# Third and fourth unit's loads behind the third block of ada, and one more row of two blocks summed on TensorE

## What is computed

```python
c_act = silu(c)
mod = c_act @ ada_w + ada_b                       # 1024 x 9216
sh1, sc1, g1, sh2, sc2, g2, sh3, sc3, g3 = split(mod, 9)
h = rms_norm(x, norm_ffn1) * (1 + sc1) + sh1
x = x + 0.5 * g1 * ((silu(h @ w_gate) * (h @ w_up)) @ w_down)
...                                               # token mixing, second feed-forward, last norm
```

## Time and profile before

| | |
|---|---|
| time, median of 3 runs | 1157.45 us (1156.35 to 1160.7) |
| time of the profiled execution | 1155.71 us |
| its span | 1153.6 us |
| PE busy | 1132.6 us, 98% of the span |
| DVE, ACT, POOL busy | 737.0, 493.1, 117.8 us |
| granted clock, mean over the span | 0.996 |

### The profile page before, as it was taken

The page is one execution under the profiler, slowest core; times in us unless marked ns, Lnnn a source line. Parts: engine busy times, 40 slices in busy tenths (PEclk is TensorE's granted clock), DMA queues, the critical chain, the costliest instruction groups (busy, mean ns, idle before and its releaser), DMA issues. The chain is left out here.

```text
span 1153.6 us, 17468 instructions
## 1 busy us (share of the span) xinstructions
PE 1132.6 (98%) x6378; PEld 989.6 (86%) x6378; DVE 737.0 (64%) x1167; ACT 493.1 (43%) x758; POOL 117.8 (10%) x115
## 2 busy tenths in 40 slices
PE   8999999999999999999999999999989999999997
PEld 6788888888888998888888888889889999978887
DVE  4766665666555666675555666757789898952332
ACT  5233332233222257665555665533545454532232
POOL 3301000000110001112011230001310101100000
PEclk9999999999999999999999999999999999999999
DMA  9567566557777425538246674341335445333331
GB/s 311 166 214 248 186 216 203 170 175 233 230 235 237 121 59 119 121 101 171 73 121 118 141 144 98 90 128 56 105 101 145 126 128 147 111 101 91 96 114 73
DMA packets 244174, 167.95 MB, mean 146 GB/s; under 512 B 6198, under 2 KB 224516, under 8 KB 244116
## 3 DMA queue, kind: packets, MB, share of 16 engines
q1 hardware_dynamic: 227188, 143.48, 41.6%
q0 software_dynamic: 16208, 21.33, 8.8%
q10 hardware_dynamic: 720, 2.36, 0.6%
HBM read 164.99 MB, written 16.05 MB: 157 GB/s over the span
## 5 line engine op out<-in xcount | busy, mean ns | idle before, releaser
L1893 PE MATMUL bank<-hH,wH 128*128 128x512 f32 (+1 forms) x976 | 355.1, 364 | 3.9 <-DVE hL L1283 3.4
L1895 PE MATMUL bank<-hH,wL 128*128 128x512 f32 (+1 forms) x976 | 351.2, 360 | 0.0
L1894 PE MATMUL bank<-hL,wH 128*128 128x512 f32 (+1 forms) x976 | 351.0, 360 | 0.0
L798 ACT ACTIVATE wH<-raw 128x1024 fp32r<-128x1024 f32 x131 | 135.8, 1037 | 351.2 <-PE bank L1895 348.4
L1217 DVE TENSOR_TENSOR wL<-raw,wH 128x1024 fp32r<-128x1024 f32 x131 | 156.7, 1196 | 201.3 <-ACT wH L798 200.4
L1893 PEld LDWEIGHTS bank<-hH,wH 128*128 128x128 f32 x976 | 184.1, 189 | 33.6 <-issue 5.4
L1895 PEld LDWEIGHTS bank<-hH,wL 128*128 128x128 f32 x976 | 184.0, 189 | 28.0
L1894 PEld LDWEIGHTS bank<-hL,wH 128*128 128x128 f32 x976 | 184.2, 189 | 26.3
L1893 PE MATMUL bank<-actH,wH 128*128 128x512 f32 (+1 forms) x316 | 120.7, 382 | 0.0
L1895 PE MATMUL bank<-actH,wL 128*128 128x512 f32 (+1 forms) x316 | 120.4, 381 | 0.0
L1894 PE MATMUL bank<-actL,wH 128*128 128x512 f32 (+1 forms) x316 | 120.4, 381 | 0.0
(11 more groups left out here) (276 smaller groups left out, 1932.6 us busy)
## 6 DMA issues: line engine op xcount, KB each, us to landing
adaw<-in_ada_w_dram SPq DMA_DIRECT2D x28, 1024.0 KB, 6.1
raw<-in_mix_w_in_dram SPq DMA_DIRECT2D x41, 512.0 KB, 3.9
raw<-in_ffn_w_down_dram SPq DMA_DIRECT2D x32, 512.0 KB, 4.0
raw<-in_ffn_w_gate_dram SPq DMA_DIRECT2D x25, 512.0 KB, 4.0
raw<-in_ffn_w_up_dram SPq DMA_DIRECT2D x25, 512.0 KB, 3.9
adas<-in_ada_w_dram SPq DMA_DIRECT2D x16, 512.0 KB, 8.2
raw<-in_ffn_w_down_dram SPq DMA_DIRECT2D x16, 384.0 KB, 4.2
wsum_d<-in_ffn_w_gate_dram POOLq DMA_DIRECT2D x8, 704.0 KB, 7.7
```

What stands on the lines that cost most here:

```text
L798: nc.scalar.activation(wH[s][:, :n * P], raw[s][:, :n * P], ACT.Copy).then_inc(hi_done, 1)
L1893: T.matmul(o, a[0], b[0], start=start, stop=False)
L1894: T.matmul(o, a[0], b[1], start=False, stop=False)
L1895: return T.matmul(o, a[1], b[0], start=False, stop=stop)
```

## The change

Four edits. On SP, the four transfers of `adas` block 2 are issued ahead of units 2 and 3. In `ROWS_PE`, blocks 1 and 2 give row 6 as well as row 7 to TensorE, so DVE has four rows of each and not five. ACT and DVE prepare units 2 and 3 later: ACT behind `hH` of tile 3, DVE behind `first_columns(2)`. On TensorE, the first tiles of units 2 and 3, which stood between `first_sums(1)` and `tiles(0, 1)`, go behind `first_parts(3)`, with 20 dummies in their old place; the order of the parts and tiles behind it changes with them.

```diff
--- before.py
+++ after.py
@@ -103,7 +103,7 @@
     ROWS_P = (2, 2, 2, 2)
 
     CHAINED = (2, 3)
-    ROWS_PE = ((6, 7), (7,), (7,), (6, 7))
+    ROWS_PE = ((6, 7), (6, 7), (6, 7), (6, 7))
     ROWS_V = [DT - len(rows) for rows in ROWS_PE]
     SUMS = [(() if b in CHAINED else (0,)) + (1,) + ((2,) if rows else ()) for b, rows in enumerate(ROWS_PE)]
     STEPS_P = [sum(2 * r - 1 for r in ROWS_P[:b]) for b in range(ADA0 + 1)]
@@ -614,9 +614,9 @@
             load_first_unit(0)
             load_first_unit(1)
             load_first_block(sp, 1)
+            load_first_block(sp, 2)
             load_first_unit(2)
             load_first_unit(3)
-            load_first_block(sp, 2)
             load_first_block(sp, 3)
             for k in range(2):
 
@@ -813,7 +813,7 @@
 
             def normed():
                 for d in range(DT):
-                    if d == 2:
+                    if d == 4:
                         for u in (2, 3):
                             first_prep(u, 0)
                     act.wait_ge(tmp_done, d + 1)
@@ -1294,12 +1294,12 @@
                 for b in range(DT // 2):
                     if b in (1, 2):
                         first_rows(b, ROWS_P[b], ROWS_V[b])
-                    if b == 1:
-                        first_prep(2)
-                        first_prep(3)
                     if b == 3:
                         first_rows(3, ROWS_P[3], ROWS_V[3])
                     first_columns(b)
+                    if b == 2:
+                        first_prep(2)
+                        first_prep(3)
                     for d in (2 * b, 2 * b + 1):
                         scaled(0, 0, d, every, B_BC[0])
                     for d in (2 * b, 2 * b + 1):
@@ -1951,19 +1951,20 @@
                 tiles(1, 0)
                 dummies(8)
                 first_sums(1)
+                dummies(20)
+                tiles(0, 1)
+                first_parts(2)
+                tiles(1, 1)
+                first_sums(2)
+                first_parts(3)
                 for u in range(2, N_FIRST):
                     tiles(u, 0)
-                tiles(0, 1)
-                tiles(1, 1)
-                first_parts(2)
-                tiles(2, 1)
-                first_sums(2)
-                tiles(3, 1)
-                first_parts(3)
-                for u in range(3):
+                    tiles(u, 1)
+                for u in range(2):
                     tiles(u, 2)
                 first_sums(3)
-                tiles(3, 2)
+                for u in range(2, N_FIRST):
+                    tiles(u, 2)
                 dummies(4, B_ADA_START[2])
                 for u in range(N_FIRST):
                     tiles(u, 3)
```

## The result

Over 20 executions of each kernel the changed one has a median of 1160.72 us (1158.9 to 1163.21) beside 1156.64 (1155.39 to 1161.39) of the kernel before. The ratio is 1.0029, with a 95% interval of 1.0019 to 1.0039: the change costs 2.2 to 4.5 us, which is real and too small to matter. (The ratio is taken over all executions; the medians alone differ by 4.1 us.) The profiled execution of the changed kernel took 1160.96 us, its span 1159.2; before it was 1155.71, 0.9 under its median, and 1153.6.

A forecast was written before the change was run, and what follows sets the result against it. TensorE, busy 98% of the span, was taken as the bound, so the start of `tiles(0, 3)`, moved from 53.93 to 56.2 us, adds 2.3 us. 1157.45 + 2.3 = 1159.7 us; range 1155.5 to 1163.

The forecast's parts named there:

- Transfers, POOL, the first wait: Block 2's first half lands by 29.4 us; POOL starts it 3.0 us earlier, its result there at 34.2, not 37.23.
- Block 1: Parts take 0.9 us more on TensorE; columns 0.8 later, `tiles(0, 1)` at 35.85, 0.4 late; 20 dummies hidden.
- Block 2, its sums and columns: TensorE's sums end at 41.55 us and, not DVE's rows, set the columns: 41.75 instead of 42.36, 0.6 early.
- `tiles(2, 0)` ~ 43.6: no wait worth a price: After block 3's parts, TensorE's first tile of unit 2 finds its preparation done at 43.6 us, with no wait priced.
- S: Start of `tiles(0, 3)`, the last stage of the first units: 53.93 us before, forecast 56.2, so +2.3 us.
- The clock: TensorE's 3.0 us of one-column sums and parts lie between two cases; half clock for 3.2 us would lose 1.6.
- Rival 1: TensorE's clock falls once, after the parts of block 3: +3.9 us in all, 1161.3 us; chance 0.18.
- Block 3: Sums up to 52.7 us, columns at 52.9 instead of 50.68, `tiles(0, 3)` 3.25 behind them at 56.2.
- What moves it moves the end by the same amount: Any shift in the start of `tiles(0, 3)`, 53.93 us before, shifts the kernel's end equally.
- Rival 2: The loop was DVE's alone; rows, POOL's wait and 0.4 of `low` leave the path: -3.2 us, 1154.3; chance 0.08.
- Rival 3: TensorE's clock stays at 1.2 GHz from the hole at 32.4 us on: +6.6 us, 1164.0; chance 0.06.
- Rival 4: Nothing: TensorE's real slack is larger than the timeline shows, 0 to +1 us, 1157.5 to 1158.5; chance 0.08.

The follow-up runs named there:

- the second profile of before: The kernel before run once more with nothing changed: 1157.09 us, ratio 0.9996.
- the last: Changed kernel with preparation ahead of block 2's columns, block 3's parts behind units 2 and 3's tiles, block 2's parts before `tiles(0, 1)`: ratio 0.9997.

## Why the prediction was right and where it failed

*The number* was 1159.7 and came out at 1160.72: no difference by 0.5%, a loss by sign and size. It came out so by the forecast's sum together with a rival to which only 0.18 was given. That it is only 1.0 off is in part luck: the base of 1157.45, a median of three, lay 0.8 above the median of 20, and the change itself was 4.1 us and not 2.3. By two signs of its own the working was wrong: a clock of 0.50 stands between 35 and 50, and TensorE waits at 44.33, where it was to run without a gap.

*Transfers, POOL, the first wait:* right. POOL starts block 2 at 28.86 (29.4 was forecast), and DVE no longer waits for it.

*Block 1:* right in effect. The columns came at 32.19, not 32.6, as the parts began 0.36 earlier (their weight loads at 26.03, and 26.39 in the earlier trace rows); `gs` gave it back (0.66 for 0.16), so that the `low` started at 35.02 (34.95) and `tiles(0, 1)` at 35.92 (35.85). The dummies took 2.35, not 2.0, under a wait that ended 1.55 after them. At the 1.2 GHz level they would not have been hidden: 20 of them took 4.4 in the second profile of before, where the prediction read some 2.9 from 7 in 1 us, a count that takes in those only partly inside.

*Block 2, its sums and columns:* right. Forecast 41.75 for the columns, measured 41.55; DVE's wait 2.25 and 2.01. That TensorE would set them and not DVE is the step on which the sign hung: the change took 1.28 us of waiting for POOL from DVE and made its waits for TensorE's sums 10 us instead of 2.7.

*"`tiles(2, 0)` ~ 43.6: no wait worth a price":* the first step that failed. The columns ahead of the preparation were priced at 0.67, with a `gs` of 0.24 in them, and `gs` took 1.08. The working asked what the earlier block 2 does to POOL but not what DVE's columns then run beside: POOL's addition for block 3. The trace of before held the warning at this very place (DVE's timeline, then POOL's):

```profile
42.76 0.24 DVE L1376 SCALAR_TENSOR_TENSOR gs<-mod,prm 128x2 f32<-128x2 f32 x1
41.70 1.28 POOL L661 TENSOR_TENSOR adasp<-sqx,adasp 128x512 f32<-128x512 f32 x1
```

There `gs` came just as the addition ended (42.98) and ended with it (43.00); columns forecast 0.6 earlier put it into the middle. This is worth 0.65 us against the forecast, as the columns came 0.2 early; the run with one POOL row gives 0.99 at S.

*The clock:* the second, and the larger. Rival 1 was what happened, in both profiles of the changed kernel and in the two others that kept its rows and its preparation behind the columns. It did not happen in the one with the preparation ahead, with the same sums and parts. The prediction weighed 3.0 us of one-column matmuls between a case that lowered the clock and one that didn't, and took the nearer. What it left out is the wait in front of dense work, which it had priced at nothing, but the run without that wait fell too. So the step that was mis-sized is the chance (0.18); the price, 1.6, was right where the low lasted 3.4 us (1.7), and short where it lasted 6.8 (2.5, from 10.7 for 8.2). And the low at 21 us says nothing of gaps: TensorE was busy at 1.00 there.

*Block 3:* from the columns to `tiles(0, 3)` 3.25 forecast, 3.26 measured (55.23 to 58.49). The 2.3 us of late columns are the two steps above.

*"What moves it moves the end by the same amount":* not borne out. S came 0.99 earlier with one POOL row and 2.6 earlier with the preparation ahead, and the ratios stayed (1.0032 and 1.0031 for 1.0029 and 1.0046). So the rows show why S is late; that S is the whole of the loss in time is not shown.

*Rival 2* (the change does what it says) fell with DVE's waits for the sums. *Rival 3* didn't come in the changed kernel, but in its order with the old rows; it cost less there than the 6.6 given, S being 56.88. *Rival 4* fell with S.

What stays open: why the times follow S so loosely. Behind S the profiles differ by 3.0 us (1099.7 to 1102.7). Two places of it are known. Near 785 us the changed kernel's TensorE waits 1.5 us for DVE's diagonals (L2002 for L1270), before 0.3; five of the seven other profiles of the changed order show it and two don't (the one with the old rows and the last), nor does any of the order of before. So this part of the loss goes with the order, though it lies behind S. A transfer to ACT that landed late stands ahead of it. Why it lands late wasn't found. The other place is the clock again, near 845 us, behind a wait of TensorE for DVE of 2.9 us before and 3.0 after. The stretch from 840 to 860, first before, then the changed kernel, then the changed kernel again:

```profile
840.00:860.00 20.00, 17.47 (x134) 17.50 (x135) 16.42 (x16) 8.43 (x10) 2.81 (x2) 0.91 0.46 132
840.00:860.00 20.00, 16.43 (x135) 16.04 (x134) 15.34 (x14) 9.75 (x11) 2.38 (x1) 1.00 0.48 138
840.00:860.00 20.00, 17.32 (x121) 17.10 (x120) 13.63 (x12) 8.68 (x10) 2.39 (x1) 0.83 0.46 133
```

The mean clock of this stretch (0.91, 1.00 and 0.83 here) is 0.91 in six of the twelve profiles, 0.83 in three and 1.00 in three, with both orders in the first two groups. Set against the first profile of before, instruction by instruction, TensorE loses some 1 us more there at 0.83 and 0.8 less at 1.00. So this part looks like scatter, and it hides the wait near 785 when only the whole stretch behind S is compared.

## What to carry to other kernels

An instruction that frees an engine is worth what the next wait on that engine leaves of it: read who ends each wait, and if it is the engine that bounds the kernel, handing it more work ahead of that wait moves the loss onto the bound. Work taken out of a hole has to be priced where it lands, at the clock and beside the engines that it finds there; a short instruction in a chain costs what runs beside it, not its own length. Try first what shortens the slow side where it stands, as one row less for POOL did here.

## What the runs showed of the hardware

**A POOL addition holds DVE's instructions.** The two-column `gs` (its inputs `mod` and `prm` both in SBUF) took 0.66, 1.08 and 1.10 us where POOL's tensor_tensor ran, each time ending within 0.03 us of it, and 0.16 without. The Trainium skill (SBUF — State Buffer, "Who interferes with whom") says that a DVE instruction with two SBUF inputs contends with a GpSimd instruction that reads SBUF, and that issue order decides who blocks. The rows of POOL's tensor_tensor agree, and so does POOL's multiplication of 2.93 us, which started behind DVE's preparation. They don't agree for that same multiplication the other way: in the same run it was still going (to 43.06) when `gs` started at 42.01 and took 0.18. Nor are multiplications harmless always: the first `low` of block 1 in the kernel before started 0.10 behind one (34.16 and 34.06) and took 1.12, where the second took 0.74. What decides is not shown.

**The clock fell behind one-column matmuls that kept TensorE busy.** In four profiles the clock went to 0.50 around 43 to 46 us, during or behind sums and parts, in two of them (45.7 and 44.6) when dense matmuls were already running, and in one (42.6) while TensorE read 1.00 busy. In the profile with the preparation ahead the same sums and parts (40.46 to 43.35) passed at 1.00, so they alone do not settle it. Where it falls differs between executions of one program: 45.7 and 42.6 for the changed kernel, and at the beginning 20.6 to 24.0 and 20.4 to 27.2 for the kernel before.
